# One core, a three-layer block: the two scan directions updated as (state + change) times decay, in place of decay times state plus decay times change

## The chip, the cores and the metric

The kernel runs on one core of a Trainium2 chip. The metric is the device time of one execution in microseconds (us). A number of runs is taken and their median is given; the profile is one execution more, with its own time.

## The reference, cut to what matters

The whole program is a hybrid layer, an attention layer and an RWKV-7 layer, each with its feed-forward part, on 512 tokens of width 1024, in float32. The change touches the recurrence of the RWKV-7 layer alone. It runs once forward and once backward over the tokens, for 16 heads of 64:

```
def step(state, inp):
    r_t, w_t, k_t, v_t, kk_t, a_t = inp
    sa = jnp.einsum('bhvk,bhk->bhv', state, -kk_t)
    state = (state * w_t[:, :, None, :] + sa[..., None] * (kk_t * a_t)[:, :, None, :]
             + v_t[..., None] * k_t[:, :, None, :])
    return state, jnp.einsum('bhvk,bhk->bhv', state, r_t)
...
for d in range(2):
    ...
    if d == 1:
        ins = [jnp.flip(t, axis=1) for t in ins]
    o = rwkv7_scan(*ins)
```

## The kernel before, in words

Every engine runs a hand-ordered program; semaphores (`wait_ge` on a named event, `then_inc` when one is done) tie them together. The RWKV layer's scan is done in chunks: 512 tokens are 8 chunks of 64, the 1024 channels are 8 blocks of 128 (two heads each). Within a chunk the recurrence is turned into matrix products, and from chunk to chunk only the state is carried.

For one block b, five pieces of work exist: a head (gates and decays), rows (transposes), a middle (a triangular inverse built in levels on TensorE, its products copied out by VectorE and ScalarE, its masks multiplied by GpSimd), an advance (the walk over the chunks) and a tail (normalisation and gating of the output). `stages` runs them as a software pipeline: while block b advances, block b - 1 has its tail, block b + 1 its middle and rows and block b + 2 its head. In what order an engine takes one piece of each is written out by hand in the string `ORDER`, one letter a piece ("a" is a piece of the advance, "m" of the middle, "t" of the tail, "h" of the head, "r" of the rows); an engine runs its queue strictly in that order. This stretch is called here the window of block b. The last block's window has its own order, in which TensorE also multiplies the layer's output weights.

The advance walks 8 steps, i = 0 to 7; in step i the forward direction is at chunk i and the backward one at chunk 7 - i, so both directions' 64 by 64 states sit side by side in one 128x128 tile `R.Sb` (128 partitions, 2 directions, 64 columns). A step has these parts:

- TensorE multiplies the old state (L2838) and VectorE adds a precomputed term: `U` (L3344).
- TensorE makes the answer from `U` (L2862), VectorE copies it out of PSUM: `SA` (L3352).
- TensorE makes the change of the state from `SA` (L2862, the "banks" written from scan_c and scan_b).
- VectorE makes the new state. Before, the decay times the old state is made early, right behind `U`, into a tile `R.Sw` (L3349, event "carried"); when the change has arrived, one scalar_tensor_tensor for each direction computes change times decay plus `R.Sw` (L3362, event "state"). The decay is one number per partition, direction and chunk (`wc`). Step 0 has no old state and uses two tensor_scalar (L3365). Step 7 needs no new state.

TensorE waits for "state" of step i - 1 before L2838 of step i, for `U` before the answer, and for `SA` before the change. In the trace all four tiles (`U`, `SA`, `Sb`, `Sw`) carry the name scan_c, and the state products' banks in PSUM are called banks.

Other lines that are spoken of: L3245 and L3239 copy products of the triangular inverse out of PSUM on VectorE, and the next product on TensorE (L2862 from scan_c, scan_a) needs them; L3232 masks products (VectorE, from PSUM); L3258 is GpSimd's product of a level mask, two SBUF inputs; L3429, L3434 and L3440 are the tail's scaling, bonus and gate on VectorE, and L3451 is GpSimd's sum of the two directions behind them, which waits for L3440; L3010 to L3046 are the head's operations on VectorE, and L3066 is the head's product on GpSimd, which waits for exponentials of ScalarE behind L3021.

Of the kernel before, what the change touches and what calls it, by code (L numbers as in the profile page):

```python
# [10 lines left out]
ALU = mybir.AluOpType  # L11
ACT = mybir.ActivationFunctionType
AX = mybir.AxisListType
P = 128
# [18 lines left out]
CH = 64  # L33
NCH = S // CH
# [3301 lines left out]
def dve_advance(g, dve, b):  # L3336
    R, o, wc = g.R, b % 2, g.R.wcs[b % 3]
    steps = g.psum_pair.rearrange("p (k x) -> p k x", k=2)
    before, answer, change = (steps[:, :, j * CH:(j + 1) * CH] for j in range(3))
    dve.wait_ge(g.at("wc", b))  # L3340
    for i in range(NCH):
        if i:
            dve.wait_ge(g.at("filled", ("as", b, i)))
            dve.e.tensor_tensor(R.U, before, R.G1[o][:, i:2 * NCH - i:2 * NCH - 1 - 2 * i, :], ALU.add).then_inc(  # L3344
                *dve.up("dve_advance", ("u", b, i)))
            if i < NCH - 1:
                dve.wait_ge(g.at("state", b, i - 1))
                w = wc.rearrange("p d c -> p (d c)")[:, i:2 * NCH - i:2 * NCH - 1 - 2 * i].unsqueeze(2).broadcast_to((P, 2, CH))
                dve.e.tensor_tensor(R.Sw, R.Sb, w, ALU.mult).then_inc(*dve.up("dve_advance", ("carried", b, i)))  # L3349
        yield  # L3350
        dve.wait_ge(g.at("filled", ("sa", b, i)))
        dve.e.tensor_copy(R.SA, answer).then_inc(*dve.up("dve_advance", ("sa", b, i)))  # L3352
        yield
        if i < NCH - 1:
            dve.wait_ge(g.at("filled", ("ds", b, i)))
            if i:
                dve.wait_ge(g.at("carried", b, i))
            for d in range(2):
                c = (i, NCH - 1 - i)[d]
                new = change[:, 1 - c % 2, :]  # L3360
                if i:
                    dve.e.scalar_tensor_tensor(R.Sb[:, d, :], new, wc[:, d, c:c + 1], R.Sw[:, d, :], ALU.mult, ALU.add).then_inc(  # L3362
                        *dve.up("dve_advance", ("state", b, i)))
                else:
                    dve.e.tensor_scalar(R.Sb[:, d, :], new, wc[:, d, c:c + 1], None, ALU.mult).then_inc(  # L3365
                        *dve.up("dve_advance", ("state", b, i)))
        yield


# [116 lines left out]
def dve_scan(g, dve, first):  # L3486
    fence(g, dve, "rwkv_in")
    dve.wait_ge(g.at("scan_consts"))
    dve.wait_ge(g.at("x_kept"))
    stages(dve, first_head(lambda b: dve_head(g, dve, b), first), lambda b: dve_rows(g, dve, b), lambda b: dve_middle(g, dve, b),  # L3490
           lambda b: dve_advance(g, dve, b), lambda b: dve_tail(g, dve, b))
    dve_last(g, dve)
# [238 lines left out]
def dve_last(g, dve):  # L3731

    b, s = NB - 2, SPLIT0["w_ro"]
    advance = dve_advance(g, dve, b + 1)

    def steps(n):
# [361 lines left out]
```

## Time and profile before

| | us |
|---|---|
| median of 3 runs | 2782.09 |
| lowest and highest | 2781.78 and 2784.73 |
| the profiled execution | 2784.2 |
| its span, first to last instruction | 2782.4 |

| engine | busy us | share | instructions |
|---|---|---|---|
| PE (TensorE matmul) | 2688.0 | 97% | 22600 |
| DVE (VectorE) | 1467.7 | 53% | 2354 |
| ACT (ScalarE) | 1220.2 | 44% | 2089 |
| POOL (GpSimd) | 387.5 | 14% | 334 |

The table gives sums over the whole span. The scan is only the stretch from about 2010 to 2386 us, so what an edit of the scan is worth has to be read there: in the timeline of single instructions, where each row gives the start, the duration, the engine, the line and, in brackets, how long the engine had been idle and what ended it.

### The profile page before, as it was taken

Reading aid. Unit: us, or ns where it says so; the run is one execution under the profiler, and the core shown is the slowest. Engines: PE = TensorE matmul, PEld = TensorE weight load, DVE = VectorE, ACT = ScalarE, POOL = GpSimd, SP = SyncE. Lnnn points to the kernel's source line nnn. Section 1 sums busy time; section 2 is a strip of 40 time slices with the busy share of each in tenths; the row PEclk is TensorE's granted clock in tenths of the full one; section 3 lists DMA queues with packets and bytes.
Section 4 is the critical chain, followed back from the end, with each engine's and each line's share of the span. In section 5 each row is a group of like instructions: output and inputs, shape, how many; then the busy total and the mean of one; then the engine's idle time right before and its main releaser. Section 6 shows DMA issues by size and latency. Waiting matters only on the chain. (4 is left out here: it accounts for less than half of the span.)

```text
span 2782.4 us, 52409 instructions
## 1 busy us (share of the span) xinstructions
PE 2688.0 (97%) x22600; PEld 2146.4 (77%) x22600; DVE 1467.7 (53%) x2354; ACT 1220.2 (44%) x2089; POOL 387.5 (14%) x334
## 2 busy tenths in 40 slices
PE   8999999999999999999999999999898988999999
PEld 6887567788888888886588888877677776788887
DVE  3535874743353333445764243596778775743343
ACT  4324763632243222324743232475566765542332
POOL 0023650000000000001200001100443543000000
PEclk9999999999999999999999999999999999999999
DMA  5222002233223232232222223222000001322231
GB/s 186 97 76 92 1 24 92 76 136 106 97 88 119 84 106 98 107 120 72 71 99 93 104 91 102 95 91 77 10 10 8 8 7 66 107 101 104 91 106 61
DMA packets 38725, 228.05 MB, mean 82 GB/s; under 512 B 4400, under 2 KB 8496, under 8 KB 14944
## 3 DMA queue, kind: packets, MB, share of 16 engines
q1 hardware_dynamic: 32576, 201.34, 21.0%
q0 software_dynamic: 5920, 23.35, 2.5%
q8 instruction: 181, 2.97, 0.4%
q14 instruction: 48, 0.39, 0.0%
HBM read 220.41 MB, written 4.26 MB: 81 GB/s over the span
## 5 line engine op out<-in xcount | busy, mean ns | idle before, releaser
L499 DVE TENSOR_TENSOR weights_lo<-ring,weights_hi 128x1024 fp32r<-128x1024 f32 x347 | 428.0, 1234 | 672.6 <-ACT weights_hi L492 667.3
L492 ACT ACTIVATE weights_hi<-ring 128x1024 fp32r<-128x1024 f32 x346 | 363.9, 1053 | 500.8 <-PE bank L721 280.7
L548 PE MATMUL bank<-h_hi,weights_hi 128*128 128x512 f32 x384 | 150.1, 391 | 0.0
L719 PE MATMUL bank<-weights_hi,mlp_p_hi 128*128 128x512 f32 x384 | 149.6, 390 | 0.0
L549 PE MATMUL bank<-h_lo,weights_hi 128*128 128x512 f32 x384 | 149.4, 389 | 0.0
L720 PE MATMUL bank<-weights_lo,mlp_p_hi 128*128 128x512 f32 x384 | 149.4, 389 | 0.0
L721 PE MATMUL bank<-weights_hi,mlp_p_lo 128*128 128x512 f32 x384 | 149.4, 389 | 0.0
L550 PE MATMUL bank<-h_hi,weights_lo 128*128 128x512 f32 x384 | 149.4, 389 | 0.0
L3258 POOL TENSOR_TENSOR scan_b<-scan_a,scan_c 128x512 f32<-128x512 f32 x96 | 124.7, 1316 | 135.6 <-DVE scan_a L3232 113.5
L548 PE MATMUL bank<-mlp_h_hi,weights_hi 128*128 128x512 f32 x336 | 130.7, 389 | 0.0
L549 PE MATMUL bank<-mlp_h_lo,weights_hi 128*128 128x512 f32 x336 | 130.7, 389 | 0.0
L550 PE MATMUL bank<-mlp_h_hi,weights_lo 128*128 128x512 f32 x336 | 130.7, 389 | 0.0
L2536 DVE TENSOR_TENSOR mlp<-mlp 128x512 f32<-128x512 f32 x64 | 44.3, 692 | 115.1 <-ACT mlp L2494 115.1
L548 PE MATMUL bank<-ffn_h_hi,weights_hi 128*128 128x512 f32 x248 | 96.5, 389 | 0.0
L549 PE MATMUL bank<-ffn_h_lo,weights_hi 128*128 128x512 f32 x248 | 96.5, 389 | 0.0
L550 PE MATMUL bank<-ffn_h_hi,weights_lo 128*128 128x512 f32 x248 | 96.5, 389 | 0.0
L548 PEld LDWEIGHTS bank<-h_hi,weights_hi 128*128 128x128 f32 x384 | 72.0, 188 | 18.6 <-issue 3.6
L721 PEld LDWEIGHTS bank<-weights_hi,mlp_p_lo 128*128 128x128 f32 x384 | 72.1, 188 | 15.1
L719 PEld LDWEIGHTS bank<-weights_hi,mlp_p_hi 128*128 128x128 f32 x384 | 72.1, 188 | 15.0 <-issue 0.2
L550 PEld LDWEIGHTS bank<-h_hi,weights_lo 128*128 128x128 f32 x384 | 72.1, 188 | 14.9
L549 PEld LDWEIGHTS bank<-h_lo,weights_hi 128*128 128x128 f32 x384 | 72.1, 188 | 14.8
L720 PEld LDWEIGHTS bank<-weights_lo,mlp_p_hi 128*128 128x128 f32 x384 | 72.1, 188 | 14.8
(845 smaller groups left out, 6881.5 us busy)
## 6 DMA issues: line engine op xcount, KB each, us to landing
ring<-in_w_m SPq DMA_DIRECT2D x64, 1024.0 KB, 4.8
ring<-in_w_mb SPq DMA_DIRECT2D x24, 1024.0 KB, 4.7
ring<-in_w_fi SPq DMA_DIRECT2D x22, 1024.0 KB, 4.8
ring<-in_w_fo SPq DMA_DIRECT2D x10, 1024.0 KB, 4.8
ring<-in_w_a SPq DMA_DIRECT2D x7, 1024.0 KB, 4.9
attn_bias<-scratch POOLq DMA_DIRECT2D x16, 448.0 KB, 4.6
ring<-in_w_rg SPq DMA_DIRECT2D x5, 1024.0 KB, 4.9
ring<-in_w_v SPq DMA_DIRECT2D x4, 1024.0 KB, 11.4
```

The source lines that it names most:

```text
L492: act.e.activation(halves(g, s)[0], raw, ACT.Copy).then_inc(*act.up("act_unit_high", ("high", s)))
L499: lane.e.tensor_tensor(lo, raw, hi.bitcast(F32), ALU.subtract).then_inc(*lane.up(f"{lane.name}_unit_low", ("low", s)))
L548: pe.e.matmul(ps[:, :], hi, xh, start=k == 0, stop=False, skip_group_check=True)
L549: pe.e.matmul(ps[:, :], hi, xl, start=False, stop=False, skip_group_check=True)
L550: m = pe.e.matmul(ps[:, :], lo, xh, start=False, stop=k == kt - 1, skip_group_check=True)
L719: pe.e.matmul(ps[:, :], xh, hi, start=k == 0, stop=False, skip_group_check=True)
L720: pe.e.matmul(ps[:, :], xh, lo, start=False, stop=False, skip_group_check=True)
L721: m = pe.e.matmul(ps[:, :], xl, hi, start=False, stop=k == kt - 1, skip_group_check=True)
L2536: dve.e.tensor_tensor(x, q, q, ALU.mult).then_inc(*dve.up("dve_squared", ("squared", layer, j, i), ("relu_read", layer, j, i)))
L3258: pool.e.tensor_tensor(R.LM[level % 2][:, u, :], R.LK[:, 0, u, :], R.lm[:, d, level, :].unsqueeze(1).broadcast_to((P, NCH, CH)), ALU.mult) ...
```

## The change

For steps 1 to 6 the early product of decay and old state is dropped. When the change has arrived, one tensor_tensor adds the old state to it for both directions, into `R.Sw`, and after a wait for that result a second tensor_tensor multiplies by the decay (broadcast along the 64 columns) into `R.Sb`. The sum is the same, (state + change) times decay. In even steps the two directions' changes lie in swapped halves of PSUM, so they are read in reverse order. Step 0 keeps its two tensor_scalar.

```
@@ -3343,10 +3343,6 @@
             dve.wait_ge(g.at("filled", ("as", b, i)))
             dve.e.tensor_tensor(R.U, before, R.G1[o][:, i:2 * NCH - i:2 * NCH - 1 - 2 * i, :], ALU.add).then_inc(
                 *dve.up("dve_advance", ("u", b, i)))
-            if i < NCH - 1:
-                dve.wait_ge(g.at("state", b, i - 1))
-                w = wc.rearrange("p d c -> p (d c)")[:, i:2 * NCH - i:2 * NCH - 1 - 2 * i].unsqueeze(2).broadcast_to((P, 2, CH))
-                dve.e.tensor_tensor(R.Sw, R.Sb, w, ALU.mult).then_inc(*dve.up("dve_advance", ("carried", b, i)))
         yield
         dve.wait_ge(g.at("filled", ("sa", b, i)))
         dve.e.tensor_copy(R.SA, answer).then_inc(*dve.up("dve_advance", ("sa", b, i)))
@@ -3354,16 +3350,16 @@
         if i < NCH - 1:
             dve.wait_ge(g.at("filled", ("ds", b, i)))
             if i:
-                dve.wait_ge(g.at("carried", b, i))
-            for d in range(2):
+                new = change[:, ::-1] if i % 2 == 0 else change
+                w = wc.rearrange("p d c -> p (d c)")[:, i:2 * NCH - i:2 * NCH - 1 - 2 * i].unsqueeze(2).broadcast_to((P, 2, CH))
+                dve.wait_ge(g.at("state", b, i - 1))
+                dve.e.tensor_tensor(R.Sw, new, R.Sb, ALU.add).then_inc(*dve.up("dve_advance", ("carried", b, i)))
+                dve.wait_ge(dve.newest)
+                dve.e.tensor_tensor(R.Sb, R.Sw, w, ALU.mult).then_inc(*dve.up("dve_advance", ("state", b, i)))
+            for d in range(2 if i == 0 else 0):
                 c = (i, NCH - 1 - i)[d]
-                new = change[:, 1 - c % 2, :]
-                if i:
-                    dve.e.scalar_tensor_tensor(R.Sb[:, d, :], new, wc[:, d, c:c + 1], R.Sw[:, d, :], ALU.mult, ALU.add).then_inc(
-                        *dve.up("dve_advance", ("state", b, i)))
-                else:
-                    dve.e.tensor_scalar(R.Sb[:, d, :], new, wc[:, d, c:c + 1], None, ALU.mult).then_inc(
-                        *dve.up("dve_advance", ("state", b, i)))
+                dve.e.tensor_scalar(R.Sb[:, d, :], change[:, 1 - c % 2, :], wc[:, d, c:c + 1], None, ALU.mult).then_inc(
+                    *dve.up("dve_advance", ("state", b, i)))
```

## Rows read from the trace of the kernel before

**Rows 1.** Stretches: us; busy PE, PEld, DVE, ACT, POOL; PEclk, DMA, GB/s.
```profile
2157.30:2206.80 49.50, 44.98 (x1416) 35.80 (x1414) 39.17 (x82) 33.27 (x55) 23.42 (x19) 1.00 0.04 10
2184.00:2200.00 16.00, 12.44 (x537) 10.91 (x536) 16.00 (x30) 9.05 (x17) 5.09 (x4) 1.00 0.02 5
```

**Rows 2.** PE's longest wait in total, 2133.1 to 2386 us: us, times, longest.
```profile
PE banks L2838 <- DVE scan_c L3362: 6.6, 10, 1.0
```

**Rows 3.** The early product in the scan: count, busy us, mean ns, idle before.
```profile
L3349 DVE TENSOR_TENSOR scan_c<-scan_c,scan_head 128x128 f32<-128x128 f32 x48 | 27.3, 568 | 0.0
```

**Rows 4.** Timeline, VectorE: two without a wait between them, two with one.
```profile
2161.50 0.29 DVE L3344 TENSOR_TENSOR scan_c<-banks,scan_b 128x128 f32<-128x128 f32 x1 [0.24 <-PE bank L2838]
2161.70 0.28 DVE L3349 TENSOR_TENSOR scan_c<-scan_c,scan_head 128x128 f32<-128x128 f32 x1
...
2176.82 0.68 DVE L3429 TENSOR_TENSOR scan_c<-scan_c 128x512 f32<-128x512 f32 x1
2177.53 1.28 DVE L3434 SCALAR_TENSOR_TENSOR scan_c<-scan_c,consts,rwkv 128x1024 f32<-128x1024 f32 x1
```

**Rows 5.** Timeline, GpSimd beside VectorE, steps 1 and 2 of block 3.
```profile
2163.08 5.42 POOL L3258 TENSOR_TENSOR scan_b<-scan_a,scan_c 128x512 f32<-128x512 f32 x4
2165.04 0.48 DVE L3362 SCALAR_TENSOR_TENSOR scan_c<-banks,scan_head,scan_c 128x64 f32<-128x64 f32 x2 [1.37 <-PE bank L2862]
2167.62 1.01 DVE L3349 TENSOR_TENSOR scan_c<-scan_c,scan_head 128x128 f32<-128x128 f32 x1
```

**Rows 6.** Timeline, step 3 of block 3 and what follows it.
```profile
2181.66 0.75 DVE L3440 SCALAR_TENSOR_TENSOR scan_c<-scan_c,consts,bank 128x512 f32<-128x512 f32 x1
2182.32 0.47 DVE L3362 SCALAR_TENSOR_TENSOR scan_c<-banks,scan_head,scan_c 128x64 f32<-128x64 f32 x2
2182.48 1.27 POOL L3451 TENSOR_TENSOR rwkv<-scan_c 128x512 f32<-128x512 f32 x1 [5.73 <-DVE scan_c L3440]
2183.14 1.29 DVE L3245 TENSOR_TENSOR scan_low<-bank,scan_head 128x512 f32<-128x512 f32 x2 [0.35 <-PE bank L2862]
2184.01 0.27 PE L2838 MATMUL banks<-scan_c,ring 64*64 64x64 f32 x2
2184.54 1.08 PEld L2862 LDWEIGHTS bank<-scan_c,scan_a 64*64 64x64 f32 x64 [0.21 <-DVE scan_low L3245]
```

**Rows 7.** The source view of L3451: duration least/median/most, first and last start.
```profile
L3451 POOL TENSOR_TENSOR rwkv<-scan_c x6: 1271/1274/1280, 2083.5 to 2333.4; 128x512 f32<-128x512 f32 x6
```

**Rows 8.** Timeline, steps 4 to 7 of block 3, VectorE, GpSimd and PE.
```profile
2188.91 0.27 PE L2838 MATMUL banks<-scan_c,ring 64*64 64x64 f32 x2 [1.01 <-DVE scan_c L3362]
2190.01 1.02 DVE L3349 TENSOR_TENSOR scan_c<-scan_c,scan_head 128x128 f32<-128x128 f32 x1
2191.82 0.46 PE L2862 MATMUL banks<-scan_c,scan_b 64*64 64x64 f32 x16
2192.04 1.26 POOL L3258 TENSOR_TENSOR scan_b<-scan_a,scan_c 128x512 f32<-128x512 f32 x1
2192.74 1.65 DVE L3024 TENSOR_TENSOR scan_head<-scan_head,rwkv 128x1024 f32<-128x1024 f32 x1
2194.71 1.21 DVE L3031 TENSOR_TENSOR scan_head<-scan_head 128x1024 f32<-128x1024 f32 x1
2199.70 0.34 PE L2862 MATMUL banks<-scan_c,scan_low 64*64 64x64 f32 x8 [0.54 <-DVE scan_c L3344]
```

**Rows 9.** Timeline, VectorE behind step 3 of block 6.
```profile
2333.61 1.28 DVE L3245 TENSOR_TENSOR scan_low<-bank,scan_head 128x512 f32<-128x512 f32 x2
```

**Rows 10.** Timeline, step 1 of block 7: the state and PE's use of it.
```profile
2362.51 0.47 DVE L3362 SCALAR_TENSOR_TENSOR scan_c<-banks,scan_head,scan_c 128x64 f32<-128x64 f32 x2 [1.27 <-PE banks L2862]
2363.38 0.27 PE L2838 MATMUL banks<-scan_c,ring 64*64 64x64 f32 x2
```

**Rows 11.** Stretches where TensorE's granted clock fell; columns as in rows 1.
```profile
2039.00:2043.00 4.00, 2.86 (x90) 2.70 (x90) 3.41 (x8) 2.13 (x6) 2.75 (x3) 0.57 0.02 4
2247.00:2255.00 8.00, 7.62 (x184) 6.98 (x183) 4.65 (x9) 1.11 (x3) 0.00 (x0) 0.57 0.01 4
```

## The prediction

> **What bounds the kernel now.** I read the table of engines first, then the stage. TensorE is busy 97% of the span, so a change in the scan counts only where TensorE waits for it; and after the scan nothing is idle enough to take a delay back, so what a window gains or loses goes to the end one for one. The busy time by stretch splits a window of 49.5 us in two [rows 1]. In its first 34 us TensorE is the bound and hardly waits. In its last 16 us VectorE is busy 16.00 of 16.00 and TensorE 12.44: there VectorE's queue sets the pace, and each microsecond put into or taken out of that queue moves the window. PE's waits name the same: from block 2's last part on, the longest in total is for the new state (L3362), 6.6 us in 10 waits [rows 2]. So two numbers decide: how late the state comes in steps 4 and 5, and how long VectorE's queue is from step 3 to step 7.
>
> **What the edit removes.** 48 early products (L3349), 27.3 us of busy time [rows 3], and the 96 scalar_tensor_tensors L3362 (6 steps of 8 blocks, two each). In the queue they cost less than their duration, since independent instructions overlap: `U` starts at 2161.50 and L3349 at 2161.70, 0.20 us later, though each takes 0.29 [rows 4]; a pair L3362 takes 0.47 [rows 6]. So an L3349 costs the queue 0.20 us, and the state is ready 0.47 after the first L3362 starts. But L3349's mean is 568 ns where an undisturbed one takes 0.28 [rows 3, 4]: some are held. At 2167.62 one takes 1.01 us, to 2168.63, and GpSimd's run of four L3258 ends at 2168.50 [rows 5]. The L3362 at 2165.04, in the middle of the same run, takes 0.48 as ever. L3349 reads two SBUF tiles; L3362 reads PSUM and SBUF. A VectorE instruction with two SBUF inputs is held until the running GpSimd instruction ends, one with a PSUM input is not.
>
> The Trainium skill has this as a rule: "SBUF — State Buffer", section "SBUF: two separate sides", says that VectorE with two SBUF inputs and GpSimd take the shared port pair as an exclusive lock, whoever starts first for the whole instruction. The trace agrees (1.01 against 0.28 us). It is the rule that speaks against this change.
>
> **What it adds.** An addition from PSUM and SBUF, 128x128, which I price as `U`, whose form it has: 0.29, not held. Then a product of the form of L3349, 0.28, which waits for the addition. The trace has no such pair of this size; a VectorE instruction that waits for the one before starts 0.03 us after its end (L3429 ends at 2177.50, L3434 starts at 2177.53) [rows 4], and GpSimd starts 0.07 after L3440 [rows 6]. I take 0.03, from the same engine: 0.59 to 0.60 us from the start of the addition to the state, against 0.47, so +0.12, at most +0.18; the next instruction follows the product's start by 0.20, again +0.12. From below the nearest row is L3349's 0.28, which makes it +0.11; a gain would need the two in less than the pair's 0.47, and no pair of rows with a wait between them comes near that.
>
> The Trainium skill says otherwise of that wait: "VectorE: DVE Perf Modes", section "The DRAIN you can't avoid", holds that the next operation doesn't start before the pipe is empty and a semaphore between costs nothing extra. By that page the four-instruction step would lose an instruction and gain nothing; here the starts are 0.20 apart without a wait and an instruction's length with one.
>
> So per step VectorE's queue gets 0.20 - 0.12 = 0.08 us shorter, and the state 0.12 us later, if nothing is held. Now the product stands on the path, and it is the kind that is held. Where it falls on a GpSimd instruction is the matter.
>
> **Where it is held: the walk through block 3.**
> - Step 1: the addition at 2165.04 stands inside the run of L3258 [rows 5], so the product waits for an L3258's end, about 0.7 us. TensorE uses that state much later, as it is the bound in this half. Price 0, hidden by TensorE's own work; without it up to 0.7 a window.
> - Step 2: no GpSimd instruction is running; +0.12, hidden likewise. L3349 was held here beside an idle VectorE; its going gains nothing.
> - Step 3: the addition starts at 2182.32. Just before it in the queue stands L3440, and GpSimd's L3451 waits for that: it starts at 2182.48, for 1.27 us, to 2183.75 [rows 6]. The product can't start before 2182.63. GpSimd is first by 0.15 us, by the order of the code and not by chance: the source view has six L3451, all 1.27 long [rows 7]. The product is held to 2183.75, the state comes at 2183.90 in place of 2182.79. TensorE uses it at 2184.01, so this is just hidden. But behind the product in VectorE's queue stand two L3245, which started at 2183.14: now 2183.82, +0.68 (0.35 of idle time ahead of them takes the rest). TensorE waited for them already (weights at 2184.54, for L3245) [rows 6]. So TensorE is 0.68 late, and VectorE's full stretch begins 0.68 late.
> - Step 4: one L3349 less, -0.20, one later state, +0.12: VectorE +0.60. TensorE waited 1.01 us for this state [rows 8], so it too is +0.60.
> - Step 5: the L3349 at 2190.01 was held too and cost the queue 0.94, until 2190.95. That goes, but VectorE can't use it: the answer and the change (its products start at 2191.82 and run 0.46) come from TensorE, which is +0.60 [rows 8]. So the addition is at 2192.9, 0.57 later than L3362 was. GpSimd's L3258 (2192.04 to 2193.30) is tied to the head's work on VectorE and shifts with it, to 2193.9. The product is held by 0.7, the state is +1.24. L3024, behind it, was held in the kernel before (1.65 against 1.21 of the like L3031 [rows 8]); now the product takes the hold in its place, and step 6's `U` is only +0.80.
> - Steps 6 and 7: -0.20 and +0.12: `U` of step 7 is +0.72, and TensorE waited for it (0.54) [rows 8]. The window ends 0.72 us later.
>
> **The sum.** The same walk for blocks 1 to 5 gives 0.67, 0.72, 0.72, 0.71 and 0.83: 3.65 us, as step 3's collision is there each time and step 5's only in some, where the longer way over TensorE gives nearly as much. Block 6 has no idle time ahead of L3245 (at 2333.61, with no idle time before it [rows 9]): the hold enters whole, +1.12, and its steps 4 and 5 wait for the state, 0.12 each: +1.36. Block 0 has no tail beside it, so no L3451: +0.12 in steps 4, 5 and 6, -0.20 once: +0.16. In block 7 in step 1 the state ends at 2362.98 and TensorE takes it at 2363.38, with weight products of the output in between [rows 10]: 0.12 is hidden in 0.40, price 0; without that cover 6 x 0.12 = 0.7. Together 3.65 + 1.36 + 0.16 = 5.17 us. The dependent wait at its upper bound adds 0.06 in some 14 steps on the path, 0.8.
>
> The profiled execution is 2784.2, of which 2782.4 is span and 1.8 lies around it; the changed kernel's would be a span of 2787.6 and a time of 2789.4. That execution is 2.1 above the median, near the highest of the three (2784.73). On the median the forecast is 2782.1 + 5.2 = 2787.3.
>
> **The rivals.**
> - *The clock.* TensorE's granted clock is 0.57 in a stretch of 4 us in block 0 and in one of 8 us in block 4 [rows 11]: time at the lower of its two levels, 1.2 in place of 2.4 GHz. Both stand in or behind the last part of a window, where TensorE waits for VectorE again and again; the last part of block 3 keeps the full clock [rows 1]. The change makes just these waits longer, by 0.7 a window. Each further fall costs 4 x 0.43 = 1.7 us to 8 x 0.43 = 3.4 us. With two more, 5.2 + 4 = 9.2: 2791.3. One more is enough to be slower. For it: the waits grow in every window, and two of seven windows fell already. Against it: five of seven didn't, and a fall may go as well as come. This rival ends on the slower side.
> - *The collision in step 3 doesn't come*, if GpSimd starts L3451 later than the 0.07 us shown, or the product isn't held in this form. Then the window enters its last part on time (0.12 goes into the idle 0.35), the hold of step 5 is what L3024 had, and steps 4 to 6 give and take 0.2 and 0.12: about 0 to -0.1 a window, 2782. Against it: six rows of L3451 behind L3440, and L3349's own holds.
> - *The relief counts in full.* This is the faster side: if nothing on the path is held and VectorE alone sets the pace, steps 4 to 6 save 0.20 + 0.94 + 0.20 - 0.36 = 0.98 a window, in five windows 4.9 us: 2777.2, and with a fall of the clock less 2775.5. Against it: in step 5 TensorE, not VectorE, brings the answer.
>
> **How the numbers follow.** A measurement can tell about 0.2%, 5.6 us, from no change. The forecast, 5.2, stands nearly on that bound, so its own case is split. Forecast (2785.5 to 2789): 0.48, of it 0.27 within and 0.21 slower. The clock: 0.20, slower. No collision in step 3: 0.22, within. Full relief: 0.10, of it 0.06 faster. Sums: slower 0.41, within 0.53, faster 0.06. The range for 8 in 10 reaches from the case without a collision, less a fall of the clock (2782 - 1.7 = 2780.3), to the clock's case and a little of its tail (2791.3 + 1): 2780.3 to 2792.3. It leaves out the full relief and a third or fourth fall of the clock.
>
> **What the profile of the changed kernel would show.** The products of the new line: those of step 3 take about 1.3 us in blocks 1 to 6 and end 0.15 after L3451; those of step 1 take some 0.9; the additions never more than 0.3. The product starts 0.03 after its addition. PE's wait for the second L3245 behind step 3 grows from 0.1 to 0.8. From L3245 to `U` of step 7 the way stays at about 16.2 us. The first 34 us of a window stay as they are. PEclk shows two low stretches. I am wrong if the products of step 3 take 0.28, if the first part of the window moves, or if the number of low stretches is another.

## The result and the profile after

The change makes the kernel a little slower, by about 0.2%. Three groups of runs, each against runs of the kernel before on the same chip:

| group | changed, us | before, us | ratio, 95% |
|---|---|---|---|
| 1 | 2789.91 | 2782.24 | 1.0024 [1.0017, 1.0032] |
| 2 | 2788.88 | 2783.34 | 1.0019 [1.0009, 1.0029] |
| 3 | 2786.39 | 2781.43 | 1.0017 [1.0009, 1.0026] |

That is +7.7, +5.5 and +5.0 us between medians. The forecast was +5.2, with 2787.3 as the time and 2780.3 to 2792.3 as the range; what counts as slower began at 5.6 us, and the first group lies above it, the two others just below. The first profiled execution was 2791.91 us with a span of 2790.1, 2.0 above the median of its runs; the profiles of groups 2 and 3 have spans of 2785.7 and 2783.7.

The table of engines shows only the bookkeeping: 48 VectorE instructions fewer, 6 us less of VectorE's time, and TensorE as before.

```profile
span 2790.1 us, 52361 instructions
PE 2688.2 (96%) x22600; PEld 2147.4 (77%) x22600; DVE 1461.3 (52%) x2306; ACT 1219.8 (44%) x2089; POOL 386.6 (14%) x334
```

The rest is read in the scan. First, how long it is. The copy `SA` is the first and the last VectorE instruction of the walk, so the source view of its line (L3352 before, L3348 after) gives the walk's length; the columns are least, median and longest duration in ns, and first and last start. Before, then the three executions of the changed kernel:

```profile
L3352 DVE COPY scan_c<-banks x64: 275/284/293, 2010.7 to 2385.3; 128x128 f32<-128x128 f32 x64
```

```profile
L3348 DVE COPY scan_c<-banks x64: 276/290/293, 2009.9 to 2393.0; 128x128 f32<-128x128 f32 x64
```

```profile
L3348 DVE COPY scan_c<-banks x64: 274/290/293, 2010.8 to 2388.6; 128x128 f32<-128x128 f32 x64
```

```profile
L3348 DVE COPY scan_c<-banks x64: 278/288/293, 2009.4 to 2386.6; 128x128 f32<-128x128 f32 x64
```

The walk takes 374.6 us before, and 383.1, 377.8 and 377.2 after. All of the difference is there: from the last `SA` to the end it is 397.1 us in all four. The clock blurs the three figures. TensorE had the lower clock for 10.2 us of the walk before [rows 11], and for 17.1, 3.4 and 3.4 us after; at most half of such a stretch is lost. Set to the 10.2 us of before, with the whole half counted, the walks are longer by 5.1, 6.6 and 6.0 us. So the first profile probably exaggerates the change, and the other two hide a part of it. The correction is rough: by it the kernel with the sum in PSUM (below; walk 376.9 us, 3.4 us of it at the lower clock) would be 5.8 us longer too, though its runs are only 1.2 us above before.

Second, what TensorE waits for in the scan (2008 to about 2390 us): total us, times, longest. Before:

```profile
PE banks L2838 <- DVE scan_c L3362: 9.3, 14, 1.0
PE banks L2862 <- DVE scan_c L3352: 6.6, 7, 1.1
PE bank L2862 <- issue: 6.2, 9, 1.7
```

After, group 1:

```profile
PE banks L2838 <- DVE scan_c L3358: 11.7, 15, 1.2
PE bank L2862 <- issue: 7.8, 9, 1.6
PE banks L2862 <- DVE scan_c L3348: 4.7, 7, 0.9
PE bank L2862 <- DVE scan_low L3245: 4.4, 6, 0.7
```

There is a new line: 4.4 us in 6 waits, 0.7 each, for L3245, the copy behind step 3. It is the same 4.4 in 6 in the profiles of groups 2 and 3. The wait for the state is longer (9.3 to 11.7; 12.0 and 13.8 in the others), the one for `SA` shorter (6.6 to 4.7).

Third, the two new instructions by group of lines (count, busy us, mean ns, idle before), which answer to [rows 3]:

```profile
L3358 DVE TENSOR_TENSOR scan_c<-scan_c,scan_head 128x128 f32<-128x128 f32 x48 | 24.4, 509 | 1.6
L3356 DVE TENSOR_TENSOR scan_c<-banks,scan_c 128x128 f32<-128x128 f32 x48 | 13.8, 288 | 42.5 <-PE banks L2862 34.3 <-PE bank L2862 8.0
```

The additions (PSUM and SBUF) take 288 ns and none over 293. The products (two SBUF inputs) have a mean of 509, with 0.29 as the undisturbed case: the early product's holds are back, now on the path. In steps 3 the profiles show 1.26 or 1.27 us six times, in step 1 0.6 to 1.2 in blocks 1 to 6.

Step 3 of block 3, the place of [rows 6], in the timeline:

```profile
2183.83 0.28 DVE L3356 TENSOR_TENSOR scan_c<-banks,scan_c 128x128 f32<-128x128 f32 x1
2183.99 1.27 POOL L3447 TENSOR_TENSOR rwkv<-scan_c 128x512 f32<-128x512 f32 x1 [5.83 <-DVE scan_c L3436]
2184.15 1.26 DVE L3358 TENSOR_TENSOR scan_c<-scan_c,scan_head 128x128 f32<-128x128 f32 x1
2185.22 1.32 POOL L3258 TENSOR_TENSOR scan_b<-scan_a,scan_c 128x512 f32<-128x512 f32 x1
2185.33 1.28 DVE L3245 TENSOR_TENSOR scan_low<-bank,scan_head 128x512 f32<-128x512 f32 x2
2186.53 0.68 DVE L3010 TENSOR_SCALAR scan_head<-scan_head 128x1024 f32<-128x1024 f32 x1
2186.76 1.26 PE L2862 MATMUL bank<-scan_c,scan_a 64*64 64x64 f32 x62 [0.74 <-DVE scan_low L3245]
2187.13 0.28 DVE L3344 TENSOR_TENSOR scan_c<-banks,scan_b 128x128 f32<-128x128 f32 x1
```

The product starts 0.16 us behind GpSimd's sum (L3451 of before, L3447 here), ends 0.15 behind it, L3245 follows at 1.50 us after the step's start where it was at 0.82, and TensorE waits 0.74. All of it is as forecast, or within 0.1 us of it. But look at L3010 and `U` (L3344), one and two lines further. Before, the same stretch was

```profile
2183.71 1.28 POOL L3258 TENSOR_TENSOR scan_b<-scan_a,scan_c 128x512 f32<-128x512 f32 x1
...
2184.34 1.19 DVE L3010 TENSOR_SCALAR scan_head<-scan_head 128x1024 f32<-128x1024 f32 x1
2185.46 0.28 DVE L3344 TENSOR_TENSOR scan_c<-banks,scan_b 128x128 f32<-128x128 f32 x1
```

L3010 was held itself, by GpSimd's L3258, from which it was let go at 2184.99. Now it comes just as that instruction ends and takes 0.68. So the queue gets 0.51 of the 0.68 us back at once: `U` stands 3.30 us after the step's start in place of 3.14, and the addition of step 4 (2189.80) at 5.97 where L3362 was at 6.00.

### The profile page after: what moved, and what is told of

Same layout as the page of the kernel before. It is cut to its first block and busy times, and to the rows that moved or that the text cites. A ratio compares the mean times of both kernels' runs of the same rounds, so it can differ in the third digit from the quotient of the medians.

```text
span 2790.1 us, 52361 instructions
## 1 busy us (share of the span) xinstructions
PE 2688.2 (96%) x22600; PEld 2147.4 (77%) x22600; DVE 1461.3 (52%) x2306; ACT 1219.8 (44%) x2089; POOL 386.6 (14%) x334
## 5 line engine op out<-in xcount | busy, mean ns | idle before, releaser
L3258 POOL TENSOR_TENSOR scan_b<-scan_a,scan_c 128x512 f32<-128x512 f32 x96 | 125.1, 1320 | 138.5 <-DVE scan_a L3232 116.5
```

Of the source, the lines that this page charges most:

```text
L3258: pool.e.tensor_tensor(R.LM[level % 2][:, u, :], R.LK[:, 0, u, :], R.lm[:, d, level, :].unsqueeze(1).broadcast_to((P, NCH, CH)), ALU.mult) ...
```

## The experiments

Each kernel is the changed one with the edit shown, but where it says otherwise. The ratios are against the kernel before.

**The changed kernel again, beside the next three.**

> The changed kernel once more, as the mark for the other runs of this chip. The theory (product held behind GpSimd's sum of the two directions in step 3, plus 0.12 us per state for the wait) gives before + 5.2 us, plus what the clock's low stretches add; the first result was + 7.7 on the medians. Expected here: 0.2 to 0.3% slower than before. Rival (the excess is the clock alone): executions with the full clock, 0.998 and above, would stand within 2 us of before.

2788.88 us, in the table above: ratio 1.0019, just under the 0.2 to 0.3% expected. Its two executions at a clock of 0.998 and 0.999 took 2785.56 and 2785.82 us, where those of the kernel before at these clocks have means of 2782.26 and 2780.17. That speaks against the clock as the only cause.

**GpSimd's sum one step later.** The sum is made to wait for step 3's new state, so that the product is first:

```
+    pool.wait_ge(g.at("state", b + 1, 3))     # ahead of GpSimd's sum of the directions
```

> The changed kernel, but GpSimd's sum of the two directions (L3451 before) waits also for the state of step 3, so it can't run when the product of step 3 starts. Theory of the hold: the products of step 3 take 0.29 us in place of 1.26, the two L3245 behind them start on time, and the time falls by 5 x 0.68 + 1.12 = 4.5 us against the changed kernel, less up to 1 us where other holds take over: 3.5 to 4.5 us faster than it. Rival (the cost is the longer way to the state, or the clock): the products get short, but the time stays within 1 us of the changed kernel.

Measured 2787.70 us, +4.4 on before: ratio 1.0015 [1.0006, 1.0023], only 1.2 us better than the changed kernel beside it, which isn't told from nothing. The 3.5 to 4.5 us of the theory didn't come. The product of step 3 is free, but the timeline of block 2 shows who has the hold now:

```profile
2135.85 0.29 DVE L3358 TENSOR_TENSOR scan_c<-scan_c,scan_head 128x128 f32<-128x128 f32 x1
...
2136.28 1.28 POOL L3448 TENSOR_TENSOR rwkv<-scan_c 128x512 f32<-128x512 f32 x1 [6.42 <-DVE scan_c L3358]
2137.52 1.28 POOL L3258 TENSOR_TENSOR scan_b<-scan_a,scan_c 128x512 f32<-128x512 f32 x1
2137.56 1.79 DVE L3010 TENSOR_SCALAR scan_head<-scan_head 128x1024 f32<-128x1024 f32 x1
```

And by group, with the same columns as above, L3010 in this kernel, in the kernel before, and in the changed one:

```profile
L3010 DVE TENSOR_SCALAR scan_head<-scan_head 128x1024 f32<-128x1024 f32 x6 | 9.6, 1604 | 0.0
```

```profile
L3010 DVE TENSOR_SCALAR scan_head<-scan_head 128x1024 f32<-128x1024 f32 x6 | 6.7, 1110 | 0.0
```

```profile
L3010 DVE TENSOR_SCALAR scan_head<-scan_head 128x1024 f32<-128x1024 f32 x6 | 4.1, 678 | 0.0
```

The sum, started later, puts off L3258 behind it in GpSimd's queue. L3258 now starts 0.04 us before L3010 and holds it for nearly all of its length: L3010 ends 0.55 us after L3258, as it did before, where it had started only 0.63 us into it. So it is L3258 that holds it in both, not the sum. The hold was not removed but handed on. It is this run that showed the error in the forecast's step 4.

**The sum kept in PSUM.** The product then has one input in PSUM and isn't of the kind that is held:

```
-    before, answer, change = (steps[:, :, j * CH:(j + 1) * CH] for j in range(3))
+    before, answer, change, kept = (steps[:, :, j * CH:(j + 1) * CH] for j in range(4))
-                dve.e.tensor_tensor(R.Sw, new, R.Sb, ALU.add)...
+                dve.e.tensor_tensor(kept, new, R.Sb, ALU.add)...
-                dve.e.tensor_tensor(R.Sb, R.Sw, w, ALU.mult)...
+                dve.e.tensor_tensor(R.Sb, kept, w, ALU.mult)...
```

> The changed kernel, but the sum of state and change is written to free columns of the same PSUM banks, so the product reads PSUM and SBUF in place of two SBUF tiles. If what holds it is the second SBUF input, no product is held, in steps 1, 3 and 5 alike: all take 0.26 to 0.30 us though GpSimd runs beside them. The time is then the changed kernel's less 4 to 5 us, so before + 0 to 3. Rival (GpSimd holds any VectorE instruction that follows, whatever its inputs): products of step 3 stay at 1.26. Second rival: writing and reading PSUM takes longer than SBUF, over 0.1 us for a pair, which would give back over 1.5 us.

Measured 2784.50 us: +1.2, ratio 1.0009 [1.0000, 1.0017], 4.4 us better than the changed kernel by the medians, 0.0010 or 2.8 us by the ratios. No product is held any more, at the same places beside the same GpSimd instructions:

```profile
L3358 DVE TENSOR_TENSOR scan_c<-banks,scan_head 128x128 f32<-128x128 f32 x48 | 14.0, 291 | 1.6
L3356 DVE TENSOR_TENSOR banks<-banks,scan_c 128x128 f32<-128x128 f32 x48 | 14.2, 296 | 39.8 <-PE banks L2862 30.2 <-PE bank L2862 9.4
```

The two instructions and the wait between them are still there, and L3010 is held again (1.19 or 1.20 us in five blocks), as nothing shifts the queue. So most of what the change costs is the hold and not the number or the wait of its instructions.

**The kernel before without the early product.** It leaves out the decay of the old state: the scalar_tensor_tensor adds the old state as it is.

```
-                dve.e.tensor_tensor(R.Sw, R.Sb, w, ALU.mult)...              # the early product
-                dve.wait_ge(g.at("carried", b, i))
+                dve.wait_ge(g.at("state", b, i - 1))
-                    dve.e.scalar_tensor_tensor(R.Sb[:, d, :], new, wc[...], R.Sw[:, d, :], ALU.mult, ALU.add)...
+                    dve.e.scalar_tensor_tensor(R.Sb[:, d, :], new, wc[...], R.Sb[:, d, :], ALU.mult, ALU.add)...
```

> The kernel before without the early product of decay and old state; the new state is change times decay plus the old state, so the old state's decay is left out of the computation, and all else stays. It prices what the removal alone can bring. My walk: 0.20 us in each of steps 4 and 6, but in step 5, where 0.94 us of queue is freed, TensorE brings the answer hardly earlier: 0.4 to 0.6 us a window, 2 to 3.5 us in all. Rival (VectorE's queue alone sets the pace of steps 4 to 6): 0.20 + 0.94 + 0.20 = 1.34 us a window, 7 us in all.

Measured 2782.99 us: -0.35, ratio 1.0001 [0.9992, 1.0010]. Both expectations missed: the rival's 1.34 us a window is excluded, and of the 2 to 3.5 us of my walk nothing is seen, though the interval leaves room for 2.2. VectorE's queue did get shorter, and TensorE's waits for the state shrank; another line grew:

```profile
PE banks L2838 <- DVE scan_c L3358: 8.7, 14, 1.0
PE bank L2862 <- issue: 8.7, 11, 1.5
PE banks L2862 <- DVE scan_c L3348: 4.7, 7, 0.9
PE banks L2862 <- issue: 2.7, 3, 1.1
```

Against before, the waits for VectorE's state and `SA` fell from 15.9 to 13.4 us, and "issue", time in which TensorE waited for nothing that the profile shows, rose from 6.2 to 8.7 on the same line. It looks as if an idle gap of VectorE's making was filled by a gap of another kind, but that isn't shown: the three profiles of the changed kernel, one and the same program, have 7.8, 7.7 and 5.8 us on that line.

**GpSimd's sum at the end of the window**, behind the head's work and step 7's `U`, where VectorE has idle time; in the changed kernel, in the kernel before, and in the one with the sum in PSUM:

```
-          "pool": "mmrmmmmmmmrtmmmttmhhmmhah"}
+          "pool": "mmrmmmmmmmrtmmmmhhmmhahtt"}
+    pool.wait_ge(g.at("u", b + 1, NCH - 1))
```

> The changed kernel, but GpSimd's sum of the two directions goes to the end of its queue in a window and waits for U of step 7, so it runs where VectorE has its idle time. Putting it merely behind the state of step 3 gave back only 1.2 us, and the trace shows why: it then held L3010 for 1.8 us. Theory (what a GpSimd instruction costs in the stretch where VectorE is full is the hold of the next two-SBUF instruction there, whichever it is): now neither the product of step 3 (0.29) nor L3010 (0.60 in place of 1.2) is held, and it comes to before - 2 us, 7 to 9 us faster than the changed kernel. Rival (the changed kernel is slow by the longer way to the state): it stays within 2 us of the changed kernel.

> The kernel before with the same move of GpSimd's sum. Theory: L3010 is held no more (0.60 in place of 1.2 us), which is 0.5 us a window in six windows: 2 to 4 us faster than before. So the difference between the changed kernel and this one's pair, both with the sum at the end, is the change without its collision: 0 to 2 us slower for the change. Rival (the sum was hidden in the kernel before, as its VectorE instruction of step 3 reads PSUM): within 1 us of before.

> Sum of state and change in PSUM, and GpSimd's sum of the directions at the end. No hold is left on the way to the state. Theory: about before - 3 us, the same as the kernel before with this move or up to 1 us better, as step 5's hold falls on L3024 and not on the product. Rival (holds on the way to the state don't matter once step 3 is free): equal to the changed kernel with the sum at the end.

Measured, with 2781.37 for the kernel before: 2782.49 (+1.1, ratio 1.0005 [0.9997, 1.0014]), 2782.67 (+1.3, 1.0002 [0.9993, 1.0011]) and 2781.94 (+0.6, 1.0003 [0.9995, 1.0012]). The gains on the kernel before that all three theories had (2 us, 2 to 4 us and 3 us) didn't come. Moving GpSimd's sum takes 4 to 6.5 us out of the changed kernel (+5.0 to +7.7 become +1.1): GpSimd's sum at its old place is the cause. The mean product falls from 509 to 392 ns, what is left being step 1's and the other holds, and L3010 is free:

```profile
L3358 DVE TENSOR_TENSOR scan_c<-scan_c,scan_head 128x128 f32<-128x128 f32 x48 | 18.8, 392 | 1.6
L3010 DVE TENSOR_SCALAR scan_head<-scan_head 128x1024 f32<-128x1024 f32 x6 | 4.1, 682 | 0.0
```

The other half of the expectation missed. In the kernel before, L3010 is freed just the same (683 ns), 0.5 us a window in the stretch where VectorE is full, and nothing comes of it. Its waits again:

```profile
PE bank L2862 <- issue: 8.8, 10, 1.7
PE banks L2838 <- DVE scan_c L3362: 8.3, 14, 0.9
```

One us less for the state, 2.6 more of "issue". None of the three is faster than the kernel before.

These kernels aren't free of holds either. At its new place the sum meets L3046, the head's last instruction on VectorE, which has two SBUF inputs; in the kernel before with the sum moved:

```profile
2199.82 2.09 DVE L3046 SCALAR_TENSOR_TENSOR scan_head<-rwkv,consts,scan_head 128x1024 f32<-128x1024 f32 x1
2202.89 0.42 DVE L3232 TENSOR_TENSOR scan_a<-bank,scan_c 128x256 f32<-128x256 f32 x1 [0.98 <-PE bank L2862]
```

It takes 2.09 us in place of 1.27. But VectorE then sits idle for 0.98 us, where at this place it had 1.64 before: this hold falls into idle time.

**The two instructions without the wait between them.** The addition adds `U` in place of the old state, and the product takes the change alone, so the old state is left out of the recurrence and neither needs the other:

```
-                dve.e.tensor_tensor(R.Sw, new, R.Sb, ALU.add)...
-                dve.wait_ge(dve.newest)
-                dve.e.tensor_tensor(R.Sb, R.Sw, w, ALU.mult)...
+                dve.e.tensor_tensor(R.Sw, new, R.U, ALU.add)...
+                dve.e.tensor_tensor(R.Sb, new, w, ALU.mult)...
```

> Prices the wait between the two instructions. The addition adds U in place of the old state, and the product multiplies the change from PSUM by the decay without waiting for the addition, so the old state is left out of the recurrence; both are 128x128 and neither is held. Against the sum kept in PSUM (2784.5), which has the wait and is not held either, this one is shorter by 0.12 us at each of the 14 to 20 states that TensorE or VectorE's queue waits for: 1.5 to 2.5 us faster than it, near before - 1. The two start 0.20 apart in place of 0.33. Rival (a wait for the own engine costs nothing): 0.33 apart here too, and the same time.

Measured 2782.52 us, +1.15, ratio 1.0004 [0.9995, 1.0013]. The kernel with the sum in PSUM had +1.2 and 1.0009 [1.0000, 1.0017] against its own runs of the kernel before. By the medians the two are alike, by the ratios this one is 1.4 us better; the 1.5 to 2.5 us expected are neither seen nor excluded. In the timeline of step 3 of block 3:

```profile
2182.06 0.28 DVE L3356 TENSOR_TENSOR scan_c<-banks,scan_c 128x128 f32<-128x128 f32 x1
2182.22 1.27 POOL L3446 TENSOR_TENSOR rwkv<-scan_c 128x512 f32<-128x512 f32 x1 [5.74 <-DVE scan_c L3435]
2182.26 0.28 DVE L3357 TENSOR_TENSOR scan_c<-banks,scan_head 128x128 f32<-128x128 f32 x1
```

Starts 0.20 apart against 0.32 with the wait, and a product with a PSUM input that starts inside GpSimd's sum and isn't held. What that is worth can't be told in the time. In the trace it can, in block 7, where no product is held: from step 3's `U` to step 7's it is 16.06 us before, 16.20 in all three profiles of the changed kernel and 16.20 with the sum in PSUM, and 16.07 here. So in that block the wait costs 0.13 us in all, not 0.12 a step.

**The new form in some steps only.** The old form stays in the others:

```
+SUM_FIRST = (3,)            # then (1, 2, 4, 5, 6), then (5,)
+            if i < NCH - 1 and i not in SUM_FIRST:   # the early product, as before
...
+            if i in SUM_FIRST:                       # addition and product
...
+            elif i:                                  # the two scalar_tensor_tensors
```

> The kernel before, with the new form of the state's update in step 3 alone, where GpSimd's sum of the two directions collides; the other steps keep the early product. If the collision of step 3 is what makes the changed kernel slower, this one has most of it: TensorE's waits for the second L3245 are 4 us in place of 0.3, and the time is 2 to 4 us above before. Rival (all steps share in it, 0.12 us each and the hold of step 5): under 1.5 us above before.

> The counterpart: the new form in steps 1, 2, 4, 5 and 6, the old one in step 3. If step 3's collision is the cause: 0 to 2.5 us above before, and with the run of step 3 alone it adds up to the changed kernel's 5.5 to 7.7. Rival: 4 us or more above before, as the changed kernel.

> The new form in step 5 alone. There the early product was held for 0.94 us and goes, and the new product is held by GpSimd's mask product (up to 0.73 us) while L3024 behind it is not held any more. By the walk of the prediction these nearly cancel: 0 to 1.5 us above before. Rival (the state is what counts, and it comes 0.5 us later in three blocks and 0.12 in the rest): the same size, so this run tells only if step 5 carries more than 2 us.

> The changed kernel again on this chip, to stand beside the three: 5 to 7 us above before.

Measured, with 2781.43 for the kernel before:

| new form in | us | more than before | ratio, 95% |
|---|---|---|---|
| step 3 | 2785.08 | 3.65 | 1.0014 [1.0005, 1.0023] |
| steps 1, 2, 4, 5, 6 | 2783.53 | 2.1 | 1.0006 [0.9997, 1.0015] |
| step 5 | 2784.26 | 2.8 | 1.0007 [0.9998, 1.0016] |
| all | 2786.39 | 5.0 | 1.0017 [1.0009, 1.0026] |

3.65 + 2.1 = 5.75 against 5.0 for all. Step 3 alone carries most of it, and of the three small kernels it alone is told from no change. The first two came as expected; step 5's 2.8 lies above the 0 to 1.5 of its expectation, and above the 2.1 of the kernel that has step 5 among its five, so some 1 us of these differences is noise. The wait that went with it is wholly there:

```profile
PE bank L2862 <- DVE scan_low L3245: 4.4, 6, 0.7
PE banks L2838 <- DVE scan_c L3372: 8.9, 14, 1.0
```

With the other five steps changed there is no such line for L3245, and the wait for the state is longer instead:

```profile
PE banks L2838 <- DVE scan_c L3365: 13.7, 14, 1.7
```

Of that 13.7, some is a state that comes while TensorE has the lower clock (10.2 us of this walk), so it isn't a clean price. The intervals of the other two small kernels include no change; what step 5 costs alone stays between nothing and 4.5 us.

## Why the prediction was right, and where it wasn't

**The size and the sign: right.** +5.2 forecast, +5.0 to +7.7 measured. A part of the excess is the clock, the rival with a chance of 0.20. Over all runs whose clock is on record (33 of the changed kernel, 97 of the kernel before, on other chips in part) the changed one has a mean granted clock of 0.9967, the other 0.9975. The means of the changed and the unchanged runs at the same clock differ by 5.2 us at 0.996, 4.5 at 0.997, 5.6 at 0.998 and 6.7 at 0.999, weighted 5.2; without regard to the clock by 6.5. So about 1.3 us go with the clock, most of it in four runs of group 1 at 0.994 and 0.995, where the kernel before has a single one. That the longer waits caused it, as the rival had it, isn't shown: 17.1, 3.4 and 3.4 us of low clock in three executions of one kernel are a wider spread than between kernels, and the kernels with the shorter waits have from 3.4 to 17.1. The forecast of two low stretches, as a mark of right or wrong, was of no use for the same reason.

**Step 3, the collision: right in each number.** Product 1.26 or 1.27 in blocks 1 to 6 (forecast 1.3), ends 0.15 after GpSimd's sum, L3245 later by 0.68 in block 3 (counted from step 3's `U` it is 0.83 in blocks 1, 3 and 5; the other 0.15 is also there, as 0.14, with step 3 in the old form and the others in the new, and wasn't followed up), TensorE's wait for it 0.74 (forecast 0.8), and the two kernels that take the hold off the path for good give 4.4 (2.8 by the ratios) and 4 to 6.5 us back. The rival without a collision is out. The rule that was weighed against the change held: the Trainium skill, "SBUF — State Buffer", section "SBUF: two separate sides", and the PSUM run is its counterpart, 291 against 509 ns.

**Step 4, "VectorE +0.60": wrong, and the mis-sized step.** The walk shifted the whole queue behind step 3 by the hold. It took L3010's 1.19 us for its own length and didn't ask whether it was held; its rows weren't among those I read. It was, by 0.51, and the shift cures that hold: +0.16 for `U` of step 4 in place of the forecast 0.68, and -0.03 for the addition in place of +0.48 (block 3; block 2 is alike). So the way from L3245 to step 7's `U`, which I had as unchanged at about 16.2 us, is shorter where nothing else interferes: in block 2 16.63 before and 15.73 or 15.74 in all three profiles, in block 1 16.37 and 15.72 in two. L3010's hold is 0.51 of these 0.90 and 0.65 us; the rest wasn't followed up. There a window costs next to nothing: from step 3's `U` to step 7's -0.07 us in block 2 and +0.15 to +0.2 in block 1 (+1.0 in the first profile), against the forecast 0.72 and 0.67.

**The sum was right because two errors met, which is luck.** Blocks 1 and 2 cost less than forecast, the late ones more. From step 3's `U` to step 7's, over the profiles without low clock there:

| block | before, us | changed, more by (in order of size) | forecast |
|---|---|---|---|
| 1 | 23.89 | 0.15, 0.2, 1.0 | 0.67 |
| 2 | 24.15 | -0.07, -0.07, -0.07 | 0.72 |
| 3 | 23.75 | 0.7, 1.1 | 0.72 |
| 5 | 24.35 | 1.2, 1.5 | 0.83 |
| 6 | 22.85 | 1.2, 2.2, 2.3 | 1.36 |

In block 6 the hold went in whole, as the walk had it: L3245 stood 0.39 us after the step's start and now stands at 1.50, +1.11 against the forecast 1.12, since no L3010 follows. What came on top of it are, for the most part, TensorE's pauses. Behind that L3245 stands one in each execution, before and then in the profiles of groups 2 and 3:

```profile
2337.37 0.74 PE L2862 MATMUL bank<-scan_low,scan_low 64*64 64x64 f32 x35 [0.47 <-issue]
```

```profile
2340.50 0.74 PE L2862 MATMUL bank<-scan_low,scan_low 64*64 64x64 f32 x35 [1.57 <-issue]
```

```profile
2338.19 0.74 PE L2862 MATMUL bank<-scan_low,scan_low 64*64 64x64 f32 x35 [0.28 <-issue]
```

1.57 and 0.28 us at one place of one kernel, and block 6 differs by 1.0 us between these two executions. My walk had no such term. In block 5 the like pause is 1.06 us before and 1.33 in both; it stands ahead of step 4's addition, which is 0.66 later there and not 0.03 earlier. Block 7, priced at 0, gave 0.14 in each profile; blocks 0 and 4 can't be read, as the clock fell in them in one profile or the other.

**Step 5: half right.** The product was held there in one, three and four of blocks 1 to 5 in the three profiles (0.48 to 1.00 us), so the 0.7 is no fixed price but depends on where L3258 happens to lie. In block 3 of group 3's profile it is held for 0.83 and L3024 behind it takes 1.21 in place of 1.65 [rows 8], the exchange that I had in the walk; the step's start was 10.03 us behind step 3's in both kernels, not 0.57 later.

**Step 1, step 2, the wait: right.** Step 1's holds of 0.6 to 1.2 us leave the first part of a window as it was: from step 7's `U` to the next block's `U` of step 3 it is 171.3 us in sum before, and 171.0, 170.6 and 170.3 after (differences of the starts of L3344, seven windows). The product starts 0.32 us after its addition, 0.03 after its end. One hold is beyond the forecast: step 2 of block 6, 1.29 us in all three, hidden. The whole relief of VectorE (0.10) is out by the run without the early product.

**What stays open.** Why the two edits of the kernel before that shorten VectorE's queue gain nothing that can be told. TensorE's pauses without a visible cause are longer in both profiles (8.7 and 8.8 us against 6.2), but that they took the gain isn't shown: with step 3 alone changed, where the waits for VectorE are longer than before, they are 8.5 us, with the sum one step later 8.0, and in the changed kernel 5.8 to 7.8. The 6.2 is one profile and may be the exception. Nothing here was done to the pauses themselves, and the intervals leave room for a gain of 2.2 and 1.9 us.

## What to carry to other kernels

When an instruction with two SBUF inputs goes on the path, look for the GpSimd instruction that its predecessor releases; here that fixed order made 1.27 us of a 0.29 us product in six windows of eight, and a PSUM operand took it away, for 3 to 4 us. Before a delay is carried along a queue, check each instruction in its way for a hold of its own (compare its duration with the shortest of its kind): holds are handed on, so a delay can cure one and a cure can make another. And a shorter queue on the second engine is worth only what the first can use: two edits of the kernel before that took VectorE's time out of the stretch where it was 16.00 of 16.00 busy bought nothing that could be told.

## What the runs showed of the hardware

- A tensor_scalar with one SBUF input (L3010, 128x1024) is held as well: 0.68 us free, 1.19 beside the second half of a GpSimd instruction of 1.28, 1.79 beside the whole of one. That one input is enough there fits the Trainium skill, the same section of "SBUF — State Buffer", which counts an operation in a two-port mode for the lock. Whether L3010 runs in such a mode no row says; its 0.68 us is about half of the 1.21 of a tensor_tensor of its size.
- When two GpSimd instructions follow one another, the waiting VectorE instruction isn't held through both: the product that starts at 2184.15 ends at 2185.41, 0.15 us after the end of the first, and the second, L3258 at 2185.22, takes 1.32 in place of 1.28.
- A product with one input in PSUM isn't held, and an addition that writes PSUM takes 296 against 288 ns.
- Two VectorE instructions with no wait between them start 0.20 us apart, with one 0.32 to 0.33. The Trainium skill, "VectorE: DVE Perf Modes", section "The DRAIN you can't avoid", has both sides of it: the semaphore costs nothing extra, and a next operation that isn't held starts earlier. ("Held" has another sense there; it isn't GpSimd that holds.) The second is what is seen here; and still the 0.12 us moved no time that could be told.
- The walk starts between 2007.7 and 2011.2 us in the profiles of kernels that are alike up to there: 3.5 us of spread that no edit of the scan makes, beside an effect of 5.0 to 7.7 us.
